# A block's differential keys and values projected by three split products instead of one fp32 product

## What is computed

```python
h = modulate(rms_norm(x, g_attn[l]), sh1, sc1)
hc = modulate(rms_norm(ctx, g_attn[l]), csh1, csc1)
qa, ka, va, qb, kb, vb = split_projection(h @ w_qkv[l])
qa_c, ka_c, va_c, qb_c, kb_c, vb_c = split_projection(hc @ w_qkv[l])
...
kb_all = jnp.concatenate([kb_c, kb], axis=1)
vb_all = jnp.concatenate([vb_c, vb], axis=1)
lat_mix = jnp.concatenate([
    gqa_attention(qa, ka_all, va_all, Q_BLOCK),
    diff_attention(qb, kb_all, vb_all, lam, diff_subln[l], lambda_init, Q_BLOCK),
], axis=-1)
x = x + gt1 * (lat_mix @ w_o[l])
x = x + gt2 * moe_ffn(modulate(rms_norm(x, g_ffn[l]), sh2, sc2), ...)
```

## Time and profile before

| | us |
|---|---|
| median of three runs | 1965.29 |
| the three runs | 1962.81, 1965.29, 1966.88 |
| the profiled execution | 1962.72 |
| its span (first to last instruction) | 1960.9 |
| TensorE busy in it | 1868.4 (95%) |
| VectorE busy | 738.2 (38%) |
| ScalarE busy | 574.9 (29%) |
| mean rate of HBM reads and writes | 287 GB/s |

### The profile page before, as it was taken

The page is one execution under the profiler, slowest core; times in us unless marked ns, Lnnn a source line. Parts: engine busy times, 40 slices in busy tenths (PEclk is TensorE's granted clock), DMA queues, the critical chain, the costliest instruction groups (busy, mean ns, idle before and its releaser), DMA issues.

```text
span 1960.9 us, 26781 instructions
## 1 busy us (share of the span) xinstructions
PE 1868.4 (95%) x10916; PEld 1179.3 (60%) x10916; DVE 738.2 (38%) x1358; ACT 574.9 (29%) x1042; POOL 525.4 (27%) x220
## 2 busy tenths in 40 slices
PE   7999999989999999999999999999999999999997
PEld 6778889977789899844584444434334443443443
DVE  4776563447855734543543212111111211111112
ACT  4544455444545454323431001101101110110111
POOL 5767656767766557200000000000000000000000
PEclk9999999999999999999989999999999999999999
DMA  8555433555544234621569999999999999999995
GB/s 308 194 193 173 150 108 121 205 178 194 202 172 169 90 130 172 225 87 43 215 266 387 427 428 428 428 428 429 428 428 428 427 427 428 428 429 429 428 428 230
DMA packets 111412, 563.37 MB, mean 287 GB/s; under 512 B 4768, under 2 KB 24352, under 8 KB 86464
## 3 DMA queue, kind: packets, MB, share of 16 engines
q1 hardware_dynamic: 111328, 562.17, 71.6%
HBM read 561.11 MB, written 1.05 MB: 287 GB/s over the span
## 4 chain that ended last, share of the span: by engine, by line
PE 63%; DMA 29%; DVE 5%; ACT 1%; issue 1%; SPq 0%; DVEq 0%; ACTq 0%
DMA ring<-in_e_in_dram 28%; PE bank L1776 15%; PE score L974 11%; PE bank L1766 10%; PE bank L776 5%; PE mixed L1012 4%; PE bank L1743 4%; PE bank L807 2%; PE mixed L1860 1%; DVE ring L2361 1%; PE flip L1843 1%; PE bank L1035 1%; PE score L995 1%; PE score L834 1%; PE mixed L856 1%
## 5 line engine op out<-in xcount | busy, mean ns | idle before, releaser
L2154 POOL TENSOR_TENSOR w_lo<-ring,w_hi 128x1024 fp32r<-128x1024 f32 (+1 forms) x216 | 525.2, 2442 | 271.3 <-ACT w_hi L2053 270.6
L974 PE MATMUL score<-ring,space 128*64 128x512 f32 x2016 | 452.8, 594 | 38.7 <-DMA ring<-in_e_in_dram 37.6
L974 PEld LDWEIGHTS score<-ring,space 128*64 128x64 f32 x2016 | 141.7, 137 | 338.7 <-issue 248.2
L2053 ACT ACTIVATE w_hi<-ring 128x1024 fp32r<-128x1024 f32 (+1 forms) x216 | 226.2, 1049 | 222.7 <-PE bank L1776 113.8
L1776 PE MATMUL bank<-h_hi,w_hi 128*128 128x256 f32 x896 | 260.3, 291 | 0.0
L1776 PE MATMUL bank<-h_lo,w_hi 128*128 128x256 f32 x896 | 252.1, 281 | 0.0
L1776 PE MATMUL bank<-h_hi,w_lo 128*128 128x256 f32 x896 | 251.0, 280 | 0.0
L1012 PE MATMUL mixed<-ring,space 128*64 128x512 f32 x1024 | 226.8, 595 | 0.3 <-ACT space L1243 0.3
L1239 ACT ACTIVATE space<-space 128x512 f32<-128x512 f32 x32 | 20.2, 631 | 696.1 <-DVE space L1549 696.1
L1549 DVE TENSOR_SCALAR space<-score 128x512 f32<-128x512 f32 x32 | 22.2, 693 | 411.5 <-PE score L974 411.5
L1776 PEld LDWEIGHTS bank<-h_hi,w_hi 128*128 128x128 f32 x896 | 168.4, 188 | 4.6 <-issue 4.4
(11 more groups left out here) (348 smaller groups left out, 2307.2 us busy)
## 6 DMA issues: line engine op xcount, KB each, us to landing
ring<-in_e_in_dram SPq DMA_DIRECT2D x126, 2048.0 KB, 25.1
ring<-in_e_out_dram SPq DMA_DIRECT2D x64, 2048.0 KB, 22.1
ring<-in_w_in_dram SPq DMA_DIRECT2D x42, 2048.0 KB, 7.8
ring<-in_w_ada_dram SPq DMA_DIRECT2D x16, 1024.0 KB, 5.2
ring<-in_w_o_dram SPq DMA_DIRECT2D x6, 2048.0 KB, 7.8
ring<-in_w_qkv_dram SPq DMA_DIRECT2D x4, 2048.0 KB, 10.0
ring<-in_w_ada_dram SPq DMA_DIRECT2D x4, 2048.0 KB, 7.9
ring<-in_w_out_a_dram SPq DMA_DIRECT2D x2, 2048.0 KB, 8.3
```

What stands on the lines that cost most here:

```text
L974: ins = pe.matmul(score[HALF * blk:HALF * blk + HALF, which * W:(which + 1) * W], xs[:, 2 * j + r, HALF * hh:HALF * hh + HALF], wk[:, blk ...
L2053: act.activation(split_part(w_hi, k), raw_part(k), ACT.Copy).then_inc(hi_done, 1)
L2154: pool.tensor_tensor(split_part(w_lo, k), raw_part(k), split_part(w_hi, k), ALU.subtract).then_inc(lo_done, 1)
```

## The change

The `kb` and `vb` units become split products. Each of their eight row chunks is now three fp32r matmuls of 512 columns (L848 of the changed kernel). `ka`, `qa` and `qb` stay fp32. For the parts:

- ScalarE rounds the two weight tiles in quarters of 128 x 1024 (`split_block`, L656): tile 3 (`kb`) after the second to fifth evacuation ahead of the loop, tile 4 (`vb`) one quarter at the end of each of steps 1 to 4.
- ScalarE rounds the two streams in four pieces (`round_stream`, L1228) just ahead of the loop.
- VectorE makes all low parts: the context stream's and half of tile 3's in step 0 ahead of that step's normalization, the rest of tile 3's behind it, the own stream's in step 1 (`low_stream`, L1463), and one quarter of tile 4's in each of steps 1 to 4, ahead of the copy of `mixed` (`low_tile`, L1455).
- The high parts of the tiles lie in slots 4 and 5, the low parts over the raw tiles, the high parts of the streams in slot 1.
- The slots of later tiles move with that, and the first expert's tiles are asked for in the order 1, 5, 3, 0, 4, 2, the first two ahead of the last two `ada` tiles.

```diff
+BLOADS = [("ka", 0, 0), ("qa", 1, 1), ("qb", 2, 2), ("kb", 3, 3), ("vb", 4, 0), ("out2", 6, 2), ("ada", 7, 3),
+          ("out2", 5, 4), ("ada", 8, 0), ("ada", 11, 3), ("ada", 12, 0)]
+BHIGH = {3: 4, 4: 5}
+BSPLIT = [3, 4]
...
+        stream_high_of = [ring_r[:, 1, i * DC * T:(i + 1) * DC * T].rearrange("p (c t) -> p c t", t=T)
+                          for i in range(2)]
+        stream_low_of = [h_hi, hc_low]
+
+        def split_block(act, i, q):
+            tl = BSPLIT[i]
+            if q == 0:
+                act.wait_ge(landed[BSLOT[tl]], barrived(tl))
+                act.wait_ge(stream_ready, LAYERS * 8)
+            act.activation(high_of(tl)[:, 2 * q:2 * q + 2, :], raw_quarter(i, q), ACT.Copy).then_inc(bhi_done, 1)
...
-            for j in (4, 5):
+            sp.wait_ge(unit_done, bdone(BLAST[3]))
+            block_tile(7)
+            block_tile(5)
+            sp.wait_ge(unit_done, bdone(BLAST[4]))
+            block_tile(8)
+            for j in (1, 5):
                 expert_tile(e_in[0], e_out[0], j)
+            for tl in (11, 12):
+                sp.wait_ge(unit_done, bdone(BLAST[{11: 7, 12: 8}[tl]]))
+                block_tile(tl)
...
-            sp.wait_ge(unit_done, bdone(NBU - 1))
-            for j in (1, 2):
+            for j, last in ((4, BLAST[5]), (2, NBU - 1)):
+                sp.wait_ge(unit_done, bdone(last))
                 expert_tile(e_in[0], e_out[0], j)
...
+                    if c % 2 == 0:
+                        pe.wait_ge(blo_done, 4 * BSPLIT.index(tl) + c // 2 + 1)
+                    if c % 4 == 0:
+                        pe.wait_ge(low_done, 2 * (1 - s_) + c // 4 + 1)
+                    x_hi, x_lo, w_h, w_l = stream_high_of[s_], stream_low_of[s_], high_of(tl), low_of(tl)
+                    for x_, w_ in ((x_hi, w_h), (x_hi, w_l), (x_lo, w_h)):
+                        ins = pe.matmul(b[:, :], x_[:, c, cols], w_[:, c, :], start=c == 0 and x_ is x_hi and w_ is w_h,
+                                        stop=c == DC - 1 and x_ is x_lo)
...
+            def round_stream(s_):
+                for piece in (slice(0, 4), slice(4, 8)):
+                    act.activation(stream_high_of[s_][:, piece, :], (h, hc)[s_][:, piece, :], ACT.Copy
+                                   ).then_inc(rounded, 1)
+
             for u in range(BFIRST - 1):
                 evacuate_block(u)
                 if u >= 2:
                     unturn(u - 2)
+                if u:
+                    split_block(act, 0, u - 1)
...
                 for u in BDONE_IN[j - 1] if j else ():
                     if u in BTURNED:
                         unturn(u)
+                if 1 <= j <= 4:
+                    split_block(act, 1, j - 1)
...
+            def low_tile(i, q):
+                tl = BSPLIT[i]
+                dve.wait_ge(bhi_done, 4 * i + q + 1)
+                dve.tensor_tensor(low_of(tl)[:, 2 * q:2 * q + 2, :], raw_quarter(i, q),
+                                  high_of(tl)[:, 2 * q:2 * q + 2, :], ALU.subtract).then_inc(blo_done, 1)
+
+            def low_stream(s_):
+                dve.wait_ge(unit_done, bdone(2 * TT - 1 if s_ else BLAST[2]))
+                for i, piece in enumerate((slice(0, 4), slice(4, 8))):
+                    dve.wait_ge(rounded, 2 * (1 - s_) + i + 1)
+                    dve.tensor_tensor(stream_low_of[s_][:, piece, :], (h, hc)[s_][:, piece, :],
+                                      stream_high_of[s_][:, piece, :], ALU.subtract).then_inc(low_done, 1)
...
+                if j == 0:
+                    low_stream(1)
+                    low_tile(0, 0)
+                    low_tile(0, 1)
+                if j == 1:
+                    low_stream(0)
                 if j < NBJ:
...
+                if j == 0:
+                    low_tile(0, 2)
+                    low_tile(0, 3)
+                if 1 <= j <= 4:
+                    low_tile(1, j - 1)
                 if j > 0:
```

More of the change, by code:

```diff
@@ L256, in build @@
         assert 2 * PARTS * 2 * W + DC * T <= (RING - LRING) * TILE
+        with nc.sbuf_tensor("ring_rounded", [P, MRING, TILE], F32R) as ring_r:
+            pass
         ring = sb("ring", [P, MRING, TILE])
@@ L275, in build @@
             latent_r = before_space.enter_context(nc.sbuf_tensor("latent_r", [P, 2 * MHEADS, T], F32R))
+        HC_AT = 9912
+        with ExitStack() as before_space:
+            before_space.enter_context(nc.sbuf_tensor("before_context", [P, HC_AT], F32))
+            hc_low = before_space.enter_context(nc.sbuf_tensor("context_low", [P, DC, T], F32R))
         space = sb("space", [P, 20888])
@@ L358, in build @@
         brope = take(2, W)
+        top[0] += -top[0] % 8
+        assert top[0] == HC_AT, top[0]
         hc = take(DC, T)
@@ L468, in build @@
         y_ready = sem("y_ready")
-        landed = [sem(f"landed{i}") for i in range(RING)]
+        landed = [sem(f"landed{i}") for i in range(MRING)]
         squared = sem("squared")
@@ L640, in block_sync, with block_tile @@
             sp.dma_start(ctx_x, ctxT).then_inc(bpar_loaded, 16)
[L641 to L655, removed]
+            def block_tile(tl):
+                src, a, width = {0: (w_qkv, W, 256), 1: (w_qkv, 0, W), 2: (w_qkv, 768, W), 3: (w_qkv, 1280, W), 4: (w_qkv, 1792, W),
+                                 5: (w_o2, 0, W), 6: (w_o2, W, W), 7: (w_ada, LAYERS * 4 * W, W),
+                                 8: (w_ada, (LAYERS * 4 + 1) * W, W), 11: (w_ada, (LAYERS * 4 + 2) * W, W),
+                                 12: (w_ada, (LAYERS * 4 + 3) * W, W)}[tl]
+                slot_ = BSLOT[tl]
+                sp.dma_start(ring[:, slot_, :].rearrange("p (c n) -> p c n", c=DC)[:, :, 0:width],
+                             columns(src, a, width)).then_inc(landed[slot_], 16)
+            sp.wait_ge(lo_done, split_count(LAYERS - 1, NQ - 1))
+            block_tile(0)
+            block_tile(1)
+            sp.wait_ge(unit_done, done(LAYERS - 1, NU - 1))
+            block_tile(2)
+            block_tile(3)
+            sp.wait_ge(unit_done, bdone(BLAST[0]))
+            block_tile(4)
+            sp.wait_ge(unit_done, bdone(BLAST[2]))
+            block_tile(6)
             def expert_tile(we, wo, j):
@@ L742, in start @@
                 tl = BUNITS[u][1]
-                before = LAYERS * 16 * NT // LRING if tl % RING < LRING else 0
-                pe.wait_ge(landed[tl % RING], before + 16 * (tl // RING + 1))
+                if tl not in BSPLIT:
+                    pe.wait_ge(landed[BSLOT[tl]], barrived(tl))
                 pe.wait_ge(bank_free[BBANK[u]], bfreed(u) - 1)
             def place(u):
-                return bank[BBANK[u]], ring[:, BUNITS[u][1] % RING, :].rearrange("p (c n) -> p c n", c=DC)
+                return bank[BBANK[u]], ring[:, BSLOT[BUNITS[u][1]], :].rearrange("p (c n) -> p c n", c=DC)
             pe.wait_ge(bsquared, 1)
@@ L1160, in block_scalar @@
             evacuate_block(BFIRST - 1)
+            for s_ in (1, 0):
+                round_stream(s_)
             def squares_of_job(j):
```

34 lines of the change are left out of this document (27 added, 7 removed).

## The result

The changed kernel takes **1970.45 us** (median of 12 runs, 1965.73 to 1972.74) against 1965.19 for the kernel before (12 runs beside it, 1962.81 to 1968.0): ratio 1.0020, 95% interval 1.0012 to 1.0028. It is slower by a little, where I had forecast 2.4 us less (called "the same"), and outside the range of 1957 to 1968. The profiled execution took 1970.31 us, with a span of 1968.5.

The account below looks back on a forecast made before the run. TensorE was taken to bound the changed stretch, its course setting the expert stream's start. Terms -11.0 + 8.6 = -2.4 us turned 1962.7 into 1960.3, or 1962.9 against the median 1965.29 ("the same"); range 1957 to 1968.

Parts of the forecast that it names:

- TensorE's saving: In steps 1 to 8, each of 16 `kb` and `vb` halves saves 0.69 us: -11.0 us in all.
- The rival of the fast pitch: The split products' matmuls run at the pitch of an undisturbed stream, -13.5 + 8.6 = -4.9 us: 1960.4; 12%.
- The new wait: Ahead of `values` in steps 2 to 5, TensorE idles 2.14 us for VectorE's copy of `mixed`: +8.6 us.
- The work ahead of the loop and in steps 0 and 1: The added roundings and subtractions on ScalarE and VectorE there make nobody wait: no cost.
- Transfers: Third `ada` tile, behind two expert tiles, arrives at 963.4, 2 us before TensorE needs it: cost nothing.
- the stalls bring TensorE's clock down: One clock fall at each of the four stalls in steps 2 to 5, +6.6 us: 1969.5; 12%.
- granted clock 1.00 from 810 to 980: Expected sign: TensorE at full clock throughout this stretch; a fall in the idle stretches would prove the forecast wrong.

Follow-up runs that it names:

- e9_early_again: Changed kernel with ScalarE rounding tile 4's quarters right behind the exponentials in steps 1 to 4, run once more: 1954.91 us, ratio 0.9957 to the kernel before.
- its repeat: The changed kernel itself, unaltered, run once more on another chip: 1968.25 us, ratio 1.0024 to the kernel before.
- kernel with two waits: Changed kernel with ScalarE's rounding of tile 4's quarter moved behind the exponentials in steps 1 and 2 only: 1963.9 us, ratio 0.9995 to the kernel before.
- kernel before with the wait: Kernel before, products still fp32, plus four unused roundings on ScalarE and subtractions on VectorE at the changed kernel's places: 1974.45 us, ratio 1.0055.
- early rounding: Changed kernel with ScalarE rounding tile 4's quarters right behind the exponentials in steps 1 to 4: first measured 1952.97 us, ratio 0.9941 to the kernel before.

## Why the prediction was wrong

- **TensorE's saving: right, 6% too large.** A half measures 2.76 to 2.80 (forecast 2.74 to 2.85), and 0.66 is saved for the 0.69 of the sum; over all steps 10.3 us are saved, for 11.0. The rival of the fast pitch is out: the matmuls of a half follow each other at 2.76 / 12 = 0.230 us, and the row of this very instruction form in the earlier trace rows was the better guide. By the 215.7 ns from start to start of the Trainium skill ("TensorE: Matmul & The Clock Gate", "Wait — 56ns, not 53.3ns?") a half would take an estimated 2.59 us; the traces of this case, with 230 ns, do not agree with it for this form of matmul.
- **The new wait: right.** Four times 2.08 for 2.14, in the steps forecast, released by the instruction forecast; 8.3 for 8.6 us. Rounding 1.05 and subtraction 1.23 stood in the rows of before as 1.06 and 1.22.
- **The work ahead of the loop and in steps 0 and 1: right.** No wait of over 0.1 us that the kernel before doesn't have.
- **Transfers: the term of nothing was mis-sized.** The third `ada` unit waits 0.2 to 0.6 us in the kernels with the changed load order:

```profile
973.18 1.06 PE L784 MATMUL bank<-ring,silu 128*32 128x512 f32 x8 [0.41 <-DMA ring<-in_w_ada_dram]
```

From the request for tile 8 (948.73) to these matmuls are 24.4 us; the sum had 22.0 to the tile's end. The late part is the transfer and not the request: the tile is asked for at 957.45, and the DMA engines are full from 952 to 973 (share 1.03, 408 GB/s). Which term was too small, the latency that I took or the 4.9 us a tile, I did not test. Worth 0.4 us.
- **The step that failed is the clock.** The sum has no term for it: I gave the rival "the stalls bring TensorE's clock down" 12% and wrote "granted clock 1.00 from 810 to 980". The runs showed a fall behind three of the four stalls, +4.7 us of the part. With that the terms are: falls +4.7, saving 0.7 too large, `ada` +0.4, stalls 0.3 too large, the stretch behind attention 0.6 shorter; 4.9 of the 5.1 us between the forecast -2.4 and the measured +2.7. The rival's mechanism, place and price (1.6 each; measured 1.55 to 1.59) were right. For four falls it gave 1969.5, but for the three that came 1967.8, inside the range. That the median lies outside takes the 2.6 us besides that the part doesn't explain; the rival's figure is near 1970.45 partly by luck. I had set against it a single row, the idle stretch of 2.15 us at 277 with the clock at 1.00 behind it. The same place in the profile of the changed kernel, with an idle time of 2.16, and a window behind it:

```profile
277.18 0.87 PE L1969 MATMUL mixed<-space 128*64 128x128 f32 x8 [2.16 <-ACT space L2141]
```

```profile
276.00:282.00 6.00, 4.82 (x30) 3.84 (x31) 2.94 (x7) 3.30 (x6) 2.36 (x1) 0.72 0.14 48
```

and in `e9_early_again`:

```profile
276.58 0.66 PE L1969 MATMUL mixed<-space 128*64 128x128 f32 x8 [2.16 <-ACT space L2141]
```

```profile
276.00:282.00 6.00, 5.42 (x47) 4.61 (x48) 2.74 (x6) 3.66 (x8) 2.40 (x1) 1.00 0.03 8
```

The same instructions, the same 2.16 us of idleness, once with a fall and once without. One execution's row says that such a stretch can pass, not that it will. Counted over the profiles of the changed kernel and its repeat, six of eight stalls brought a fall; with the two stalls left in the kernel with two waits and the four in the kernel before with the wait, ten of fourteen. The row that I had quoted in favour of the rival, the standstill of 2.17 us in the earlier trace rows with 0.50 some 6 us later in the earlier trace rows, I had misread: the 2.17 are those of the weight loads. TensorE's matmuls stood still for 1.29 at that place:

```profile
980.75 0.63 PE L844 MATMUL flip<-cst,space 128*128 128x128 f32 x4 [1.29 <-DVE space L1395]
```

All 13 profiles of this study have this stop, and nine have a low stretch behind it (the second column of the table). So the rows of before held one place where an idle stretch passed without a fall and one where a shorter one had a low stretch behind it. "Two of four stalls" would have been the fair reading: -2.4 + 3.2 = +0.8 for the sum and 1966.1 for the median, and a range that reaches beyond four falls.
- **What stays open.** The part explains +2.7 of +5.3 us (and +3.3 of +4.8 in the repeat). In the profiles of this study the block starts between 809.21 and 814.67 us. All 13 have a low stretch in the layers near 413 to 421. Beside it the two at 809.21 and 809.34 show none between 200 and 800; five at 812.0 to 812.6 show one or two, and four at 814.2 to 814.7 show three. Both profiles of kernels built on the kernel before (810.10, 809.26) show none; of eleven built on the changed one, two show none and nine start at 812.0 or later. That may be chance: no engine's instruction ahead of the block differs. That the layers' clock falls more often in the changed kernel is not excluded, and was not tested; it would be worth about 2 us. The mean granted clock of all runs gives it no support: 0.9916 in the 53 runs of the kernels built on the changed one that leave TensorE no idle stretch of 2.1 us in attention, and 0.9912 in the 52 of the kernel before beside them. It is taken over the whole span, so it can't settle the question.

## What to carry to other kernels

A stall on TensorE may cost more than its idle time: before an edit that opens short idle stretches in front of long matmul work is priced, add one clock fall to each (here 1.6 us on a stall of 2.1, in ten of fourteen cases) as the likely case, and judge by several executions whether a place can be idle without one. Read a standstill from the matmuls' rows, not from those of the weight loads. When an engine in between makes low parts for another engine, put the copy that TensorE waits for ahead of them, or make what they need early: here the order of two lines turned medians 8 to 11 us under the kernel before into one 5 over it. Where a stall can't be removed, matmuls whose result is overwritten can hold the clock and pay for themselves.

## What the runs showed of the hardware

- TensorE's clock fell to the 1.2 GHz level behind idle stretches of 2.08 to 2.16 us in some executions and not in others, at one and the same place of one and the same instruction stream; ten of fourteen times in the block's stalls, six of eight of them in the changed kernel. A fall cost 1.55 to 1.59 us of fp32r matmuls and 1.7 of fp32 ones.
- Nine fp32r matmuls (2.33 us) in each of four such stretches kept the granted clock at 1.00 from 875 to 920, and took 4.5 us off the stretch from the first scores to the transposes of step 15.
- The idle stretch of 1.3 us in step 2 of the early rounding had no fall behind it: the granted clock is 1.00 in its windows from 871 to 920. Behind attention, where TensorE's matmuls stand still for 1.29 and then 0.72 us, nine of 13 profiles have a low stretch and four have none; the same work takes 12.9 to 14.3 us with it and 11.3 without.
